# Expert blocks' outputs added to the residual in HBM by indirect DMA, in place of a buffer of blocks and a final sum

## The reference

```python
h2 = modulate(rmsnorm(x1, norm2_g), sh2, sc2)
# top-1 of 4 groups, then top-2 of its 8 experts; w = the two weights
order = argsort(e_flat)                       # 4096 slots sorted by expert
padded = (counts + 127) // 128 * 128          # each expert's slots fill blocks of 128
yb = run_block(h2[buf_tok])                   # per block: (silu(x @ w1[e]) * (x @ w3[e])) @ w2[e]
moe = zeros.at[buf_tok].add(yb * buf_w)       # each token gets the rows of its two slots
out = x1 + g2 * moe
```

## Time and profile before

| | before |
|---|---|
| median of 3 runs | 3327.38 us (3325.04 to 3334.97) |
| profiled execution, own time | 3326.76 us |
| its span | 3324.9 us |
| mean granted TensorE clock | 0.932 |
| busy: PE, DVE, ACT, POOL | 86%, 59%, 46%, 9% |
| moved by DMA | 596.56 MB |
| expert loop | about 2332 to 3231 us |

### The profile page before, as it was taken

How to read it: one execution, slowest core, us unless ns; L and a number is a source line. 1 busy time by engine, 2 the same in 40 slices (tenths; PEclk the granted TensorE clock), 3 DMA queues, 4 the chain that set the end, 5 groups by cost and what they waited for, 6 DMA issues and landing times. The chain is left out here.

```text
span 3324.9 us, 41753 instructions
## 1 busy us (share of the span) xinstructions
PE 2874.6 (86%) x13558; PEld 2235.0 (67%) x13559; DVE 1965.0 (59%) x2995; ACT 1526.5 (46%) x2459; POOL 312.3 (9%) x231
## 2 busy tenths in 40 slices
PE   2699898999999996889995988993999999999990
PEld 2576676676767675777774766883777777777760
DVE  5547895545545454544454562225677777777776
ACT  3314454555555452222233331220677777777770
POOL 3101121000000001110110001110101010100103
PEclk8899998999999998898897998995999999999995
DMA  5273425333333325211128985523978978765857
GB/s 211 67 238 146 137 80 145 109 111 108 111 111 105 105 105 197 67 46 40 47 75 295 299 267 201 206 102 117 328 264 297 389 279 284 256 236 202 292 194 309
DMA packets 334109, 596.56 MB, mean 179 GB/s; under 512 B 32025, under 2 KB 134681, under 8 KB 330018
## 3 DMA queue, kind: packets, MB, share of 16 engines
q1 hardware_dynamic: 307458, 527.17, 46.5%
q0 software_dynamic: 11664, 42.47, 3.5%
q10 hardware_dynamic: 14864, 25.33, 2.0%
HBM read 433.42 MB, written 161.50 MB: 179 GB/s over the span
## 5 line engine op out<-in xcount | busy, mean ns | idle before, releaser
L2529 DVE TENSOR_TENSOR moe_w_lo<-moe_W,moe_w_hi 128x1024 fp32r<-128x1024 f32 x392 | 461.5, 1217 | 38.8 <-ACT moe_w_hi L2452 38.1
L2452 ACT CAST moe_w_hi<-moe_W 128x1024 fp32r (+1 forms) x392 | 407.3, 1054 | 91.0 <-PE moe_h3b L2382 35.1
L1670 PE MATMUL project_bank<-h_lo,w_hi 128*128 128x512 f32 x512 | 203.8, 398 | 0.0
L694 DVE TENSOR_SCALAR_CACHE_REDUCE att_S<-att_bank 128x512 f32<-128x512 f32 x192 | 125.0, 689 | 121.7 <-PE att_bank L482 121.7
L515 PE MATMUL att_bank<-h_hi,w_hi 128*128 128x512 f32 x384 | 171.6, 447 | 12.3 <-PEq L137 9.0
L2407 PE MATMUL moe_yb<-moe_W,moe_hT 128*128 x384 | 172.6, 592 | 0.0
L2380 PE MATMUL moe_h1b<-moe_w_hi,moe_xT_hi 128*128 128x512 f32 x384 | 157.6, 410 | 3.8 <-DVE moe_xT_lo L2540 3.8
L600 ACT ACTIVATE att_S<-att_S,att_nm 128x128 f32<-128x128 f32 (+15 forms) x128 | 154.1, 1206 | 0.0
L516 PE MATMUL att_bank<-h_lo,w_hi 128*128 128x512 f32 x384 | 153.5, 400 | 0.0
L2381 PE MATMUL moe_h1b<-moe_w_lo,moe_xT_hi 128*128 128x512 f32 x384 | 153.1, 399 | 0.0
L517 PE MATMUL att_bank<-h_hi,w_lo 128*128 128x512 f32 x384 | 152.9, 398 | 0.0
(11 more groups left out here) (458 smaller groups left out, 6977.5 us busy)
## 6 DMA issues: line engine op xcount, KB each, us to landing
moe_W<-in_moe_w SPq DMA_DIRECT2D x96, 2048.0 KB, 10.4
w_raw<-in_gate_w SPq DMA_DIRECT2D x48, 512.0 KB, 3.7
out_sg<-gateT SPq DMA_DIRECT2D x32, 768.0 KB, 8.2
ybuf<-moe_y ACTq DMA_DIRECT2D x48, 512.0 KB, 7.2
ybuf<-att_zero SPq DMA_DIRECT2D x36, 512.0 KB, 6.6
gateT<-att_gates SPq DMA_DIRECT2D x48, 256.0 KB, 2.5
gateT<-gate_out SPq DMA_DIRECT2D x48, 256.0 KB, 2.3
front_w<-in_ada_w SPq DMA_DIRECT2D x8, 1024.0 KB, 7.5
```

Source lines behind the costliest of these rows:

```text
L1670: pe.matmul(bank[n % 4][:], w_hi[b][:, k, :], low[:, k, at], start=False, stop=False)
L2452: nc.scalar.copy(w_hi[:, slot(p, first), :], raw(at, p)).then_inc(q["w13_high"], 1)
L2529: nc.vector.tensor_tensor(w_lo[:, own, :], raw(at, p), w_hi[:, own, :].bitcast(F32), ALU.subtract).then_inc(q["w1_low" if p < 4 else "w3_l ...
```

## The change

- `x1` and `ybuf` are gone. The output projection writes x1 into `acc`, a tensor of 2048 + 128 rows in HBM, and each block's output is added to it by an indirect DMA with addition.
- `place_y` moves to DVE, between the last low pieces and `split_h`, and multiplies by the slot's weight and by g2 at once.
- POOL's turn becomes `gather(i + 2)` and then `add_rows(i)`: copy the column of row numbers, wait for `y_placed`, issue the DMA, wait until it has landed, and only then go on. Slots that fill a block up add to one of 128 spare rows, a row of its own for each partition.
- When all is added, SP copies `acc` to the output with four DMAs from HBM to HBM. The 32 gathers, DVE's 48 operations, the loads of x1 and the 16 stores are gone.
- The 36 stores of zeros in attention are gone; one store of zeros to the spare rows comes after the loop over the heads, and the stage waits for it.
- The one-hot products take token numbers and weights side by side, 132 columns at once, into one bank: 2 x 16 = 32 products where there were 64.
- The loads of experts 1 and 2 wait for `blk_made` and for the landing of the first gather.

```diff
@@ attention, SP
-                        if u == 2:
-                            clear_late_blocks(sp, g, zero, h, q["cleared"])
                 sp.wait_ge(q["raw_ready"], 16 * HEADS * CH)
-                sp.wait_ge(q["cleared"], 16 * LATE * HEADS)
+                sp.dma_start(g["acc"][T:T + P, :].rearrange("p (a n) -> p a n", n=P), zero[:].unsqueeze(1).broadcast_to([P, KD, P])).then_inc(q["cleared"], 16)
+                sp.wait_ge(q["cleared"], 16)
@@ stage_moe, SP
-                sp.wait_ge(q["slots_made"], 1)
                 sp.wait_ge(q["blk_made"], 3)
+                sp.wait_ge(x_ready, 16)
...
-                load_x1(NE - 3, 0)
-                load_x1(NE - 2, 1)
                 for n in parts:
                     sp.wait_ge(ready[n], NE * 16)
-                for i in range(NT):
-                    sp.wait_ge(q["added"], i + 1)
-                    sp.dma_start(o_t[:, i, :], x1_tile(i)).then_inc(q["out_stored"], 16)
+                sp.wait_ge(q["finished"], 2)
+                for i in range(4):
+                    rows = slice(i * (T // 4), (i + 1) * (T // 4))
+                    sp.dma_start(g["out"][0][rows, :].rearrange("(p a) n -> p (a n)", p=P),
+                                 g["acc"][rows, :].rearrange("(p a) n -> p (a n)", p=P)).then_inc(q["out_stored"], 16)
@@ PE
                 for a in range(2):
                     pe.wait_ge(q["hot"], a + 1)
-                    for v in range(2):
-                        for t in range(NT):
-                            mm = pe.matmul(yb[v][:, 0:NBK], slot_hot[a][:, t, :], block_hot[a][v][:, t, :], start=a + t == 0, stop=a * NT + t == 2 * NT - 1)
+                    for t in range(NT):
+                        mm = pe.matmul(yb[0][:, 0:2 * NBK], slot_hot[a][:, t, :], block_hot[a][:, t, :], start=a + t == 0, stop=a * NT + t == 2 * NT - 1)
@@ DVE (the same on ACT, with the store, is gone)
+                def place_y(b):
+                    dve.wait_ge(q["block_done"], b + 1)
+                    dve.wait_ge(q["y_free"], b + 1)
+                    for nh in range(2):
+                        part = slice(nh * 512, nh * 512 + 512)
+                        nc.vector.scalar_tensor_tensor(y[:, part], yb[nh][:], slot_w[:, bass.ds(b, 1)], row[:, part], ALU.mult, ALU.mult).then_inc(q["y_placed"], 1)
...
                     low_13(b + 1, at, range(3, R))
+                    place_y(b - 1)
                     split_h(b)
@@ POOL
+                def add_rows(b):
+                    nc.gpsimd.tensor_copy(to_row[:], slot_row[:, bass.ds(b, 1)]).then_inc(q["row_copied"], 1)
+                    pool.wait_ge(q["y_placed"], b * 2 + 4)
+                    pool.sem_inc(q["gathering"], 1)
+                    pool.wait_ge(q["row_copied"], b + 1)
+                    pool.sem_inc(q["gathering"], 1)
+                    pool.indirect_dma_start(out=g["acc"], out_offset=bass.IndirectOffsetOnAxis(ap=to_row[:, 0:1], axis=0), in_=y[:],
+                                            in_offset=None, compute_op=ALU.add).then_inc(acc_added, 16)
+                    pool.wait_ge(acc_added, b * 16 + 16)
+                    pool.sem_inc(q["y_free"], 1)
...
                 with pool.Fori(0, count) as i:
                     gather(i + 2)
+                    add_rows(i)
...
+                add_rows(count)
```

More of the change, by code:

```diff
@@ L326, in stage_front @@
         s.end()
[L329 to L337, removed]
 def gate_plan():
@@ L1830, in stage_merge_out @@
     x_t = g["x"][0].rearrange("(t p) n -> p t n", p=P)
-    x1_t = g["x1"].rearrange("(t p) n -> p t n", p=P)
+    x1_t = g["acc"][0:T, :].rearrange("(t p) n -> p t n", p=P)
     h2_t = g["h2"].rearrange("(t p) n -> p t n", p=P)
@@ L2199, in stage_moe @@
     NBK = NB_OUT
-    x1_t = g["x1"].rearrange("(t p) n -> p t n", p=P)
-    o_t = g["out"][0].rearrange("(t p) n -> p t n", p=P)
     R, PW, P13, P2, KS = 5, 1024, 8, 2, 2
@@ L2217, in stage_moe @@
         slot_w = s.sb("slot_w", [P, NBK])
-        slot_tok = s.sb("slot_tok", [P, NBK], U32)
+        slot_tok, slot_row = s.sb("slot_tok", [P, NBK], U32), s.sb("slot_row", [P, NBK], U32)
+        to_row = s.sb("to_row", [P, 1], U32)
+        rest, tokens_f = s.sb("rest", [P, NBK]), s.sb("tokens_f", [P, NBK])
+        next_tok, spare_row = s.sb("next_tok", [P, NT]), s.sb("spare_row", [P, 1])
         room = [SLOT]
@@ L2235, in stage_moe @@
         slot_hot = [scratch(NT, P) for _ in range(2)]
-        block_hot = [[scratch(NT, NBK) for _ in range(2)] for _ in range(2)]
+        block_hot = [scratch(NT, 2 * NBK) for _ in range(2)]
         assert room[0] <= W2_AT
@@ L2241, in stage_moe @@
         names = ("w13_high w2_high w1_low w3_low w2_low used block_done idx_copied x_turned x_high x_split "
-                 "gated silued hidden h_turned h_high h_split y_placed go gathering finished stored "
-                 "dve_done shifted exped diffed exped2 counted ranked owned owners hot slots_made blk_made y_summed y_scaled added row_ready out_stored").split()
+                 "gated silued hidden h_turned h_high h_split y_placed go gathering finished "
+                 "dve_done shifted exped diffed exped2 counted ranked owned owners hot slots_made blk_made row_ready row_copied y_free out_stored").split()
         q = {n: s.sem(n) for n in names}
@@ L2246, in stage_moe @@
         x_ready = s.kept_sem("x_ready")
[L2247 to L2259, removed]
+        acc_added = s.kept_sem("acc_added")
         def blocks_left(eng):
@@ L2317, in next_2 @@
                     load("w2", e, u)
[L2319 to L2325, removed]
                 for n in parts:
@@ L2351, in _ @@
                     next_2(e, e % SLOTS2)
-                load_x1(NE - 3, 0)
-                load_x1(NE - 2, 1)
                 for n in parts:
                     sp.wait_ge(ready[n], NE * 16)
-                for i in range(NT):
-                    sp.wait_ge(q["added"], i + 1)
-                    sp.dma_start(o_t[:, i, :], x1_tile(i)).then_inc(q["out_stored"], 16)
-                sp.wait_ge(q["out_stored"], NT * 16)
+                sp.wait_ge(q["finished"], 2)
[3 more added lines that the diff above has]
+                                 g["acc"][rows, :].rearrange("(p a) n -> p (a n)", p=P)).then_inc(q["out_stored"], 16)
+                sp.wait_ge(q["out_stored"], 64)
             @block.tensor
@@ L2475, in place_h @@
                     nc.scalar.copy(hT[:].rearrange("p k n -> p (k n)"), htb[:, KS * P:]).then_inc(q["h_high"], 1)
[L2477 to L2483, removed]
                 act.wait_ge(q["shifted"], 1)
                 nc.scalar.activation(eg, eg, ACT.Exp).then_inc(q["exped"], 1)
-                act.sem_inc(q["y_placed"], 2)
-                act.sem_inc(q["stored"], 16)
                 high_13(0, 0, 0, range(R), first=True)
@@ L2512, in _ @@
                     high_13(b + 1, at, e, range(3, R))
-                    place_y(b - 1)
                     place_h(b)
@@ L2518, in _ @@
                     high_2(count, e, k)
-                place_y(count)
-                act.wait_ge(q["stored"], count * 16 + 32)
-                act.sem_inc(q["finished"], 1)
             @block.vector
@@ L2630, in _ @@
                 link(nc.vector.tensor_copy(in_block, of_block))
+                link(ts(next_tok[:], const(g, "tok"), 1.0, None, ALU.add))
+                link(ts(spare_row[:], const(g, "tok")[:, 0:1], float(T + 1), None, ALU.add))
                 for a in range(2):
-                    tokens, weights = block_hot[a]
+                    tokens, weights = block_hot[a][:, :, 0:NBK], block_hot[a][:, :, NBK:2 * NBK]
                     shape = [P, NT, NBK]
@@ L2635, in _ @@
                     link(tt(weights, tokens, over(r["wt"][:, a, :], shape), ALU.mult))
-                    link(tt(tokens, tokens, over(const(g, "tok"), shape), ALU.mult))
+                    link(tt(tokens, tokens, over(next_tok[:], shape), ALU.mult))
                     tt(slot_hot[a], const(g, "blk").unsqueeze(1).broadcast_to([P, NT, P]), over(in_slot[:, a, :], [P, NT, P]),
@@ L2643, in _ @@
                 dve.wait_ge(q["hot"], 3)
-                link(nc.vector.tensor_copy(slot_tok[:], yb[0][:, 0:NBK]))
-                nc.vector.tensor_copy(slot_w[:], yb[1][:, 0:NBK]).then_inc(q["slots_made"], 1)
+                link(ts(tokens_f[:], yb[0][:, 0:NBK], 1.0, None, ALU.subtract))
+                ts(slot_tok[:], tokens_f[:], 0.0, None, ALU.max).then_inc(q["slots_made"], 1)
+                link(ts(rest[:], tokens_f[:], 0.0, spare_row[:, 0:1], ALU.is_lt, ALU.mult))
+                link(nc.vector.tensor_copy(slot_w[:], yb[0][:, NBK:2 * NBK]))
+                tt(slot_row[:], rest[:], tokens_f[:], ALU.add).then_inc(q["slots_made"], 1)
                 dve.wait_ge(q["blk_made"], 3)
+                dve.wait_ge(q["row_ready"], 16)
                 count = blocks_left(dve)
@@ L2677, in _ @@
                     low_2(count, e, k)
[L2678 to L2687, removed]
+                place_y(count)
             @block.gpsimd
```

(13 more changed lines are left out.)

## The result

The changed kernel takes 3685.41 us (median of 4, 3681.94 to 3690.54) against 3328.78 for the kernel before (now the median of 4): a ratio of 1.1071, with an interval of 1.1049 to 1.1092. It is slower by 11%, 20 us beyond the predicted 3665 and inside the range. The profiled execution took 3685.7 us, its span 3683.9, which is 359.0 more than before.

The account below looks back on a forecast made before the run. PE was taken to set the pace in the expert loop. Against 3326.8 us, +313 +81 -42 -13.5 +0.5 -3.4 +2.5 = +338 gave 3665 us, with an 8-in-10 range of 3400 to 3900.

Parts of the forecast that it names:

- POOL's queue: Expert loop: the next gather queues behind the add's landing, so PE stalls 6.8 us in the mean, 46 times: +313 us.
- the fixed part: Expert loop, last product to next turn_x: evacuations, notices and issues besides the two transfers, 3.5 us a block.
- A: Expert loop: the indirect add from issue to landing, taken as 6 us alone and 9 among loads.
- G: Expert loop: the gather from issue to landing, 5.0 us unloaded and 7.8 loaded.
- The two kinds of block: Expert loop: two thirds of blocks among weight loads, stalling 8.7 us; the rest unloaded, stalling 2.9 us.
- The clock: Expert loop: after 8.7 us stalls PE runs at half rate, 2.65 us in two thirds of 46 blocks: +81 us.
- The rule against it: Rival in the expert loop: both transfers, 3.2 us each by formula, fit the gap without stall; 3271 us, chance 7%.
- DVE's new work: Expert loop: output evacuation moved from ACT to DVE, 1.28 us in a 3.42 us hole; free without PE stalls.
- The tail: After block 47: last add, then an 8.39 MB copy at 409 GB/s, 20.5 us: -42 us, or 22 gained.
- One-hot products: Before the expert loop: 64 instructions of 132 columns at 0.22 us replace 128 at 0.215: -13.5 us, bounds 0 and -20.
- Later loads: Loads of experts 1 and 2 start after the first gather, which drops from 8.69 to 5.3 us: -3.4 us.
- Attention: End of attention: one store of spare rows behind the last gate store lengthens the stage's end: +2.5 us (0 to 4).

Follow-up runs that it names:

- the gather first: The changed kernel with POOL's turn reordered, gather(i+3) ahead of add_rows(i), one gather more in all: 3269.46 us, 0.9819 of the kernel before.

## Why the prediction was right, step by step

- **POOL's queue: +313 predicted, +317 measured.** Right in place, in the wait and in count (46). That the sum comes so near is in part luck, since errors in it cancel. By the chain of waits the fixed part was 4.07 us at the least and 4.3 in the mean, not 3.5 (some +37 us over 46 blocks): in the period shown it is 2.5 us from PE's last product to the add's issue (2.3 predicted), 1.5 from landing to the gather's issue (1.2) and 0.05. A was 7.5 in the mean where two thirds at 9 and one third at 6 make 8.0 (-24 us), and G 6.7 where 6.9 was taken (-7 us).
- **The two kinds of block were not the predicted ones.** I had two thirds of the blocks with both transfers among loads, a stall of 8.7 us, and one third with both alone, 2.9. Measured: A is 5.9 to 7.0 us in 28 of 46 blocks, 8.4 to 8.8 in 9 and 9.9 to 10.2 in 9; G is 4.3 to 9.3. In many blocks only one of the two was slow, as in the period before the `turn_x` at 3216:

```profile
3199.03 6.38 DMA acc<-moe_y,moe_to_row
...
3206.98 9.01 DMA moe_x<-h,moe_idx
```

The stalls are 3.7 to 9.9 us, none under the predicted 2.9 and the longest over the 8.7. In the period shown above 4.07 + 9.94 + 7.46 - 11.62 = 9.85, and PE's longest wait is 9.9. That the wait is the cause is shown from both sides: taken away (3269) and put into the kernel before (3657).

- **The clock: +81 predicted, +98 less the 7 that stay, so about +91, measured.** The mechanism was right and the term was sized low, in the number of blocks: I had counted no fall behind the short stalls, but the clock was down in all 46 blocks. The transposes took 1.97 us in 42 of them and 1.20 to 1.69 in the other four, behind stalls of about 4 us, where 0.87 is full clock, and `turn_x` and product 2 together took 1.5 to 2.9 us more than the 7.10 of before: 101 us in all, 2.2 a block, against 2.65 in two thirds of the blocks. The Trainium skill, page "TensorE: Matmul & The Clock Gate", section on HAM oscillation, says that a loop waiting for a DMA each turn starts cold every time; the trace agrees with it, in 46 blocks of 46.
- **The rule against it.** The Trainium skill, page "DMA: Bandwidth & Descriptors", section on the anatomy of one SWDGE DMA, gives a formula from which 3.2 us is the estimate for each of the two transfers; by it nothing would have stalled. Scatters with addition took 5.9 us at the least here, and gathers 4.3: the measurement decides.
- **DVE's new work: 0 predicted, 0 measured.** With the gather first, the loop runs at 18.73 us a block with `place_y` on DVE; DVE has 86 of 100 us instead of 77.
- **The tail: -42 predicted, -36.6 measured.** The mis-sized term is the copy. Its packets run from 3653.8 to 3680.6 us, 26.7 us for 8.39 MB or 314 GB/s, where I had 20.5 at 409; the window shown, with 292, also holds the 1.4 us before the first packet. From the first issue (3652.43) to the end of the span it is 31.4 us and not 20.5 + 6.1 = 26.6. The gain was between the two ends that I gave.
- **One-hot products: -13.5 predicted, -17.6 in the trace.** That a product of 132 columns would cost about what one of 66 did was right: 12 in 2.74 us at a clock of 0.50, 0.23 each, where the 66 took 0.215. That the clock would rise midway I had only as a bound.
- **Later loads: -3.4 predicted, -4.1 in the trace** of the changed kernel; by itself too little to be told from none.
- **Attention: +2.5 predicted, +1.5 measured.** From the issue of the last gate store to the next stage's first DMA it was 6.5 us before (1243.85 to 1250.34) and is 8.0 now, as SP's timeline of the changed kernel shows:

```profile
1246.39 0.34 SPq L423 DMA_DIRECT2D gateT<-att_gates  x1
1246.77 0.94 SPq L449 DMA_DIRECT2D acc<-att_zero  x1
1254.43 0.55 SPq L902 DMA_DIRECT2D late_hi<-late_hi  x1
```

The terms of the loop fell short by 21 us together (394 predicted, 415 measured) and the tail's gain by 5; the other terms came out some 6 us better. That is the 20 us between 3665 and 3685.

## What to carry to other kernels

Before an operation with a wait is put into a queue, look at what comes behind it there and when that is wanted: here a gather with 16.7 us to spare was put behind a transfer that could not start until 7 us of these were gone, and the same two operations in the other order make the kernel 1.8% faster instead of 11% slower. Two transfers one behind the other have to be priced at what such transfers take in the trace among the others, not alone. A stall of PE costs more than its length: here stalls of 3.7 to 9.9 us cost about 2 us each on top, in products at half clock.

## What the runs showed of the hardware

- Products of plain fp32 with 66 columns, one behind the other for 27.6 us, never raised the granted clock from 0.50; the same with 132 columns raised it after about 5 us, with PE busy in the trace in both. So half as many products, each of twice the columns, took 10.0 us in place of 27.6.
- An indirect scatter of 512 KB with addition took 1.5 us more than without, in the median (6.5 and 5.0); 0.6 of that is POOL's own instruction (1.60 and 0.99).
- In all 46 stalls of PE in the loop, of 3.7 to 9.9 us, the granted clock fell from 1.00 to 0.50: during the wait, or, behind four stalls of 3.8 to 4.1 us, during the transposes that followed it.
- A copy from HBM to HBM moved 311 to 323 GB/s while it ran, with packets of 4 or of 64 KB, where gathers and stores between HBM and SBUF moved 409.
